# Expert weights fetched as pairs: one 2 MB transfer with 16 KB per partition in place of two of 1 MB

## The chip, the cores and the metric

The kernel runs on one core of one Trainium2 chip. The metric is the device time of one execution in microseconds (us). Before the change it is 2197.31 us, the median of three runs (2195.88, 2197.31 and 2199.11 us). For this kernel a difference of less than about 0.2% (4.4 us) can't be told from none.

## What is computed

The reference is a stack of transformer blocks over 256 tokens of width 1024, in float32. The first block has two layers. Each layer runs a hybrid mixer (latent attention, retention and a causal block attention) and then a feed-forward part: layer 0 a dense SwiGLU of inner width 2816, layer 1 a mixture of eight SwiGLU experts of inner width 3584. The second block follows with a feed-forward, a gated mixer with dilated attention, a cross attention to 256 memory rows and another feed-forward. The part that the change touches is this one:

```python
def moe_swiglu(x, w_router, w_gate, w_up, w_down):
    logits = (xt @ w_router).astype(jnp.float32)
    top_v, top_i = lax.top_k(logits, TOP_K)          # TOP_K = 2 of 8 experts
    top_w = jax.nn.softmax(top_v, axis=-1)
    ...
    for e in range(N_EXPERTS):
        y = y + gates[:, e:e + 1] * swiglu(xt, w_gate[e], w_up[e], w_down[e])
```

All eight experts' weights are read: 8 x 3 x 1024 x 3584 floats, 352 MB.

## The kernel before

All weights are laid out on the host as one stream of 504 chunks. A full chunk is a tile of 128 partitions x 2048 float32 (`CW`), 8 KB per partition and 1 MB in all. Chunks 72 to 407 (`AT["f1"]` is 72, `3 * U_MOE` is 336) are the experts': each expert has 14 units of 256 inner columns, and a unit takes three chunks, two that hold gate and up columns and one that holds down rows.

A chunk goes through four engines, in this order:

- SyncE (`load`, lines 345 to 349) brings chunk n into slot n % 6 of `raw` (`RAW` = 6 slots). It first waits until VectorE is done with chunk n - 6 (`lo_done`). The transfer's arrival adds 16 to the semaphore `landed` of that slot. In a feed-forward stage SyncE runs a loop whose body issues six transfers.
- ScalarE (`hi`, lines 1121 to 1125) waits for `landed` and for TensorE to be done with chunk n - 3 (`used`), and writes the rounded copy into slot n % 3 of `whi`.
- VectorE (`lo`, lines 1492 to 1496) subtracts that from the raw chunk into `wlo`, the remainder, and adds one to `lo_done`, which frees the raw slot.
- TensorE multiplies in three passes (`mm3`, lines 483 to 486): high by high, high times remainder and remainder times high. In the experts' stage a chunk is four 128 x 512 blocks, so twelve matmuls.

Within a unit (`unit` inside each engine's `experts`) TensorE runs `gate_up` on two chunks, `down` of the unit before on the third, and `turn`, two transposes (line 657) of the unit's activated product. ScalarE's order is: `hi` of two chunks, the SiLU (line 1227) once `gate_up` is done, `hi` of a third chunk, the copy of the transposed product (line 1233). VectorE's order is: `lo` of two chunks, the product (line 1647), `lo` of the third, the remainder of the transposed product (line 1653). All of these orders are fixed in the program, so what stands behind a waiting `hi` on ScalarE, or behind a waiting `lo` on VectorE, waits too. ScalarE and VectorE run two chunks ahead of the chunk that TensorE is at (`LEAD` = 2).

GpSimd brings the gathered token rows of each next expert in (`xs`, 512 KB) and stores the outputs of each one before (512 KB), on its own queue.

Of the kernel before, what the change touches and what calls it, by code (L numbers as in the profile page):

```python
# [24 lines left out]
P = 128  # L25
# [4 lines left out]
CW = 2048  # L30
RAW = 6
# [5 lines left out]
LB = 3 * UNROLL  # L37
# [18 lines left out]
U_MOE = NE * U_E  # L56
# [68 lines left out]
AT, WIDTH = {}, []  # L125
# [64 lines left out]
    raise KeyError((stage, kind))  # L190


class Chunk:


    def __init__(self, base, it=0):
        self.raw = base % RAW
        self.split = base % SPLIT
        self.width = WIDTH[base]
        self.base = base  # L200
        self.n = base + LB * it
        self.landed = 16 * (base // RAW + 1) + (16 * (LB // RAW)) * it


def in_chunk(l, c):

    return AT[f"in{l}"] + c if c < 4 else AT[f"inb{l}"] + c - 4
# [14 lines left out]
def program(nc, stream, x_in, mem_in, pos_in, consts, route_in, cols_in, rows_in, ws_in, blank_in, out):  # L222
    with ExitStack() as ctx:
        def sb(name, shape, dt=F32):
            return ctx.enter_context(nc.sbuf_tensor(name, shape, dt))
# [3 lines left out]
        def sem(name):  # L229
            if name not in sems:  # L230
                sems[name] = ctx.enter_context(nc.semaphore(name))
            return sems[name]
# [24 lines left out]
        raw = sb("raw", [P, RAW, CW])  # L257
# [53 lines left out]
        a = 2 * T * D  # L311
# [21 lines left out]
        landed = [sem(f"landed{n}") for n in range(RAW)]  # L333
        hi_done = sem("hi_done")
        lo_done = sem("lo_done")
# [8 lines left out]
        @block.sync  # L344
        def _(sp):
            def load(c):
                if not (isinstance(c.n, int) and c.n < RAW):
                    sp.wait_ge(lo_done, c.n - RAW + 1)
                sp.dma_start(raw[:, c.raw, 0:c.width], stream[c.n, :, 0:c.width]).then_inc(landed[c.raw], 16)

            for t in range(T):
                sp.wait_ge(sem(f"x_in{t}"), 16)
            n = 0
            while n < NCHUNK:
                if any(n == AT[f] for f in ("f0", "f1", "f2", "f3")):
                    name = next(f for f in ("f0", "f1", "f2", "f3") if n == AT[f])
                    loops = 3 * (U_MOE if name == "f1" else U_FF) // LB
                    with sp.Fori(0, loops) as it:
                        for j in range(LB):
                            load(Chunk(n + j, it))  # L360
                    n += loops * LB
                else:
                    load(Chunk(n))
                    n += 1
# [746 lines left out]
        def _(act):  # L1111
# [7 lines left out]
                act.wait_ge(sem("act_chain"), chained[0])  # L1119

            def hi(c):
                act.wait_ge(landed[c.raw], c.landed)
                if not (isinstance(c.n, int) and c.n < SPLIT):
                    act.wait_ge(used, c.n - SPLIT + 1)
                act.activation(whi[:, c.split, 0:c.width], raw[:, c.raw, 0:c.width], ACT.Copy).then_inc(hi_done, 1)  # L1125

            def advance(upto):

                while cursor[0] <= min(upto, NCHUNK - 1):
                    hi(Chunk(cursor[0]))  # L1130
                    cursor[0] += 1
# [45 lines left out]
            def ffn(name, units, scaled=None):  # L1177
                first_chunk = AT[name]

                def unit(u, base, it, chunks):  # L1180

                    n = base + LEAD
                    for j in range(chunks - 1):
                        if n + j < NCHUNK:
                            hi(Chunk(n + j, it))
                    act.wait_ge(used, base + LB * it + 2)
                    for t in range(T):
                        act.activation(sg[:, t, :], ps[t][:, 0:FU], ACT.Silu,  # L1188
                                       scale=rstd[:, t:t + 1] if scaled else 1.0).then_inc(unit_sem(name, "sg"), 1)
                    if n + chunks - 1 < NCHUNK:  # L1190
                        hi(Chunk(n + chunks - 1, it))
                    act.wait_ge(*at(name, "ut", u + 1))
                    act.activation(hth[:, 0:2, :], ps[2][:, :].rearrange("p (k s) -> p k s", k=2), ACT.Copy).then_inc(  # L1193
                        unit_sem(name, "hh"), 1)
# [186 lines left out]
            for l in range(DEPTH):  # L1381
# [12 lines left out]
                else:  # L1394
                    act.wait_ge(sem("rt_flag"), 1)
                    overfull = act.value_load(flag[0:1, 0:1], min_val=0, max_val=1)
                    n = cursor[0]
# [41 lines left out]
            for t in range(T):  # L1439
                m = act.activation(prob[:, t, :], r[:, t, 512:D], ACT.Square, accum_out=ss[:, 2 + t:3 + t])  # L1440
# [24 lines left out]
            for i in range(X_H):  # L1465
# [3 lines left out]
                for t in range(T):  # L1469
                    m = act.activation(prob[:, i % 2, t * S:(t + 1) * S], ps[2 + i % 2][:, t * S:(t + 1) * S], ACT.Exp,  # L1470
                                       bias=nmax[:, i, t:t + 1], scale=X_D ** -0.5, accum_out=rsum[:, i, t:t + 1])
# [727 lines left out]
def lay_out_stream(a):  # L2199

    big = np.zeros((NCHUNK, P, CW), np.float32)

    def project(name, w):
        n = AT[name]
        for c in range(0, w.shape[1], 512):
            part = w[:, c:c + 512]
            wide = part.shape[1]
            v = part.reshape(KD, P, wide).transpose(1, 0, 2)
            if wide == 512:
                big[n] = v[:, 0:4].reshape(P, CW)  # L2210
                big[n + 1] = v[:, 4:8].reshape(P, CW)
                n += 2
            else:
                big[n, :, 0:KD * wide] = v.reshape(P, KD * wide)
                n += 1

    def ffn(name, gate, up, down):

        units = gate.shape[0] * gate.shape[2] // FU
        per = units // gate.shape[0]  # L2220
        first_chunk = AT[name]
        for u in range(units):
            e, c = u // per, (u % per) * FU
            gu = np.concatenate([gate[e, :, c:c + FU].reshape(KD, P, FU), up[e, :, c:c + FU].reshape(KD, P, FU)], axis=2)
            v = gu.transpose(1, 0, 2)
            first = first_chunk + max(3 * u - 1, 0)
            big[first] = v[:, 0:4].reshape(P, CW)
            big[first + 1] = v[:, 4:8].reshape(P, CW)
            last = first_chunk + (3 * u + 4 if u < units - 1 else 3 * u + 2)
            big[last] = down[e, c:c + FU].reshape(2, P, D).transpose(1, 0, 2).reshape(P, CW)  # L2230

    first = np.cumsum([0, 256, 128, 32] + [320] * 7)
    parts = dict(zip(("ret q", "ret k", "ret v", "gate", "moba q", "moba k", "moba v"), first[3:]))

    def head_columns(part, n):
        return np.arange(parts[part] + HD * n, parts[part] + HD * (n + 1))

    order = [np.arange(C_PAIR)]
    for pair in PAIRS:
        order += [head_columns(f"{kind} {part}", n) for part in "qkv" for kind, n in pair]  # L2240
    order = np.concatenate(order + [head_columns("gate", n) for n in range(RET_H)])
    for l in range(DEPTH):
        w = a["w_in"][l][:, order]
        c = 0
        for g, wide in enumerate(IN_WIDTHS):
            v = w[:, c:c + wide].reshape(KD, P, wide).transpose(1, 0, 2)
            c += wide
            for j in range(2):
                big[in_chunk(l, 2 * g + j), :, 0:4 * wide] = v[:, 4 * j:4 * j + 4].reshape(P, 4 * wide)
        big[AT[f"uq{l}"], :, 0:1152] = a["w_uq"][l].reshape(2, P, 576).transpose(1, 0, 2).reshape(P, 1152)  # L2250
        big[AT[f"ukv{l}"], :, 0:768] = a["w_ukv"][l]
        v = a["w_o"][l].reshape(KD, P, D).transpose(1, 0, 2)
        n = AT[f"o{l}"]
        for part in range(2):
            big[n + part, :, 0:1536] = v[:, 0:3, 512 * part:512 * part + 512].reshape(P, 1536)
        big[n + 2] = v[:, 3:5].reshape(P, CW)
        big[n + 3] = v[:, 5:7].reshape(P, CW)
        big[n + 4, :, 0:1024] = v[:, 7]
    ffn("f0", a["ffn_w_gate"], a["ffn_w_up"], a["ffn_w_down"])
    big[AT["router"], :, 0:KD * NE] = a["router"][0].reshape(KD, P, NE).transpose(1, 0, 2).reshape(P, KD * NE)  # L2260
    ffn("f1", a["exp_w_gate"][0], a["exp_w_up"][0], a["exp_w_down"][0])
    ffn("f2", a["ffn1_w_gate_2"], a["ffn1_w_up_2"], a["ffn1_w_down_2"])
    project("in2", a["w_in_2"][0])
    project("out2", a["w_out_2"][0])
    project("wk", a["cross_wk_2"][0])
    project("wv", a["cross_wv_2"][0])
    project("wq", a["cross_wq_2"][0])
    project("xo", a["cross_wo_2"][0])
    ffn("f3", a["ffn2_w_gate_2"], a["ffn2_w_up_2"], a["ffn2_w_down_2"])
    return big  # L2270
# [35 lines left out]
```

## Time and profile before

| | us |
|---|---|
| median of three runs | 2197.31 |
| the profiled execution's own time | 2198.82 |
| its span, first to last instruction | 2197.0 |
| TensorE matmul busy | 2051.8 (93% of the span) |
| VectorE busy | 1516.8 (69%) |
| ScalarE busy | 1246.8 (57%) |
| weights' DMA queue (q1), share of 16 engines' span | 63.0% |

The times above come from one profiled execution. The page of the profile also has the span in 40 equal slices of 55 us. The experts' stage fills slices 10 to 27, about 540 to 1490 us from the start, and there the slices of the DMA engines read 9 tenths nearly throughout. Matmuls overlap in the records (each is listed as some 0.39 us long while the next one starts 0.23 us after it), so TensorE's busy time says whether it stands still and not how fast it could be.

### The profile page before, as it was taken

Reading aid. Unit: us, or ns where it says so; the run is one execution under the profiler, and the core shown is the slowest. Engines: PE = TensorE matmul, PEld = TensorE weight load, DVE = VectorE, ACT = ScalarE, POOL = GpSimd, SP = SyncE. Lnnn points to the kernel's source line nnn. Section 1 sums busy time; section 2 is a strip of 40 time slices with the busy share of each in tenths; the row PEclk is TensorE's granted clock in tenths of the full one; section 3 lists DMA queues with packets and bytes.
Section 4 is the critical chain, followed back from the end, with each engine's and each line's share of the span. In section 5 each row is a group of like instructions: output and inputs, shape, how many; then the busy total and the mean of one; then the engine's idle time right before and its main releaser. Section 6 shows DMA issues by size and latency. Waiting matters only on the chain.

```text
span 2197.0 us, 26792 instructions
## 1 busy us (share of the span) xinstructions
PE 2051.8 (93%) x9606; PEld 1700.9 (77%) x9606; DVE 1516.8 (69%) x1528; ACT 1246.8 (57%) x1302; POOL 67.8 (3%) x84
## 2 busy tenths in 40 slices
PE   6979998986999999899989999998999988989997
PEld 6858886876888888788878888876888766877886
DVE  5664455656889899799979899996555554545543
ACT  5544434544777777677767777765444543434443
POOL 1010000001000000000000000220000000000000
PEclk9989999996999999999999999998999977999999
DMA  7336554334999999899989999996555421434550
GB/s 306 125 129 245 188 174 141 116 116 164 374 370 388 375 381 380 331 371 383 374 336 378 380 375 364 406 362 224 195 190 191 163 106 69 161 106 153 191 191 19
DMA packets 78375, 548.77 MB, mean 250 GB/s; under 512 B 8960, under 2 KB 8960, under 8 KB 15840
## 3 DMA queue, kind: packets, MB, share of 16 engines
q1 hardware_dynamic: 72576, 519.77, 63.0%
q0 software_dynamic: 5712, 27.77, 3.4%
q8 instruction: 64, 1.05, 0.2%
q14 instruction: 23, 0.19, 0.0%
HBM read 540.68 MB, written 10.49 MB: 251 GB/s over the span
## 4 chain that ended last, share of the span: by engine, by line
PE 89%; DVE 6%; ACT 3%; issue 1%; DMA 1%; POOL 0%; DVEq 0%; ACTq 0%; SPq 0%; POOLq 0%
PE ps L484 27%; PE ps L486 27%; PE ps L485 27%; DVE wlo L1495 1%; PE ps L657 1%; ACT whi L1125 1%; PE ps L592 1%; PE ps L500 1%; DVE resid L1542 0%; PE ps L853 0%; DMA raw<-in_stream 0%; PE ps L874 0%; DVE r L1551 0%; DVE xtl L1509 0%; PE ps L742 0%
## 5 line engine op out<-in xcount | busy, mean ns | idle before, releaser
L1495 DVE TENSOR_TENSOR wlo<-raw,whi 128x2048 fp32r<-128x2048 f32 (+3 forms) x504 | 1142.6, 2271 | 370.0 <-ACT whi L1125 364.5
L1125 ACT ACTIVATE whi<-raw 128x2048 fp32r<-128x2048 f32 (+3 forms) x504 | 950.1, 1887 | 261.2 <-PE ps L486 256.8
L484 PE MATMUL ps<-whi,xth 128*128 128x512 f32 (+2 forms) x1872 | 748.9, 400 | 28.6 <-DVE wlo L1495 9.9
L486 PE MATMUL ps<-whi,xtl 128*128 128x512 f32 (+2 forms) x1872 | 729.5, 390 | 0.0
L485 PE MATMUL ps<-wlo,xth 128*128 128x512 f32 (+2 forms) x1872 | 728.4, 389 | 0.0
L484 PEld LDWEIGHTS ps<-whi,xth 128*128 128x128 f32 x1872 | 357.3, 191 | 101.8 <-issue 21.9
L486 PEld LDWEIGHTS ps<-whi,xtl 128*128 128x128 f32 x1872 | 356.6, 191 | 72.3
L485 PEld LDWEIGHTS ps<-wlo,xth 128*128 128x128 f32 x1872 | 357.9, 191 | 65.3
L484 PE MATMUL ps<-whi,hth 128*128 128x512 f32 (+2 forms) x736 | 287.4, 390 | 6.7 <-DVE htl L1607 4.5
L486 PE MATMUL ps<-whi,htl 128*128 128x512 f32 (+2 forms) x736 | 286.2, 389 | 0.0
L485 PE MATMUL ps<-wlo,hth 128*128 128x512 f32 (+2 forms) x736 | 285.1, 387 | 0.0
L484 PEld LDWEIGHTS ps<-whi,hth 128*128 128x128 f32 x736 | 138.6, 188 | 36.3 <-issue 5.6
L486 PEld LDWEIGHTS ps<-whi,htl 128*128 128x128 f32 x736 | 138.4, 188 | 28.2
L485 PEld LDWEIGHTS ps<-wlo,hth 128*128 128x128 f32 x736 | 138.7, 188 | 27.3
L1227 ACT ACTIVATE prob<-ps 128x256 f32<-128x256 f32 x112 | 43.1, 385 | 92.2 <-PE ps L486 92.2
L1233 ACT ACTIVATE hth<-ps 128x256 fp32r<-128x256 f32 x112 | 43.1, 384 | 85.8 <-PE ps L657 85.8
L1193 ACT ACTIVATE hth<-ps 128x512 fp32r<-128x512 f32 x33 | 19.7, 598 | 101.0 <-PE ps L592 101.0
L500 PE MATMUL ps<-cst,resid 128*128 128x128 f32 x112 | 24.0, 384 | 53.6 <-DVE resid L1542 51.5
L500 PEld LDWEIGHTS ps<-cst,resid 128*128 128x128 f32 x112 | 19.2, 199 | 58.7 <-DVE resid L1542 42.3
L1188 ACT ACTIVATE prob<-ps,rstd 128x256 f32<-128x256 f32 x44 | 18.4, 470 | 79.0 <-PE ps L486 79.0
L1607 DVE TENSOR_TENSOR htl<-ps,hth 128x512 fp32r<-128x512 f32 x33 | 22.8, 691 | 52.4 <-ACT hth L1193 52.4
L1647 DVE TENSOR_TENSOR probt<-prob,ps 128x256 f32<-128x256 f32 x112 | 46.5, 415 | 2.8 <-ACT prob L1227 2.8
(318 smaller groups left out, 1295.2 us busy)
## 6 DMA issues: line engine op xcount, KB each, us to landing
raw<-in_stream SPq DMA_DIRECT2D x481, 1024.0 KB, 6.6
raw<-in_stream SPq DMA_DIRECT2D x8, 768.0 KB, 4.4
bc<-in_rows POOLq DMA_DIRECT2D x5, 1024.0 KB, 5.1
slot_rows<-in_blank POOLq DMA_DIRECT2D x7, 512.0 KB, 9.5
kc<-slot_rows POOLq DMA_DIRECT2D x7, 512.0 KB, 8.6
sum_rows<-r POOLq DMA_DIRECT2D x7, 512.0 KB, 8.1
raw<-in_stream SPq DMA_DIRECT2D x4, 832.0 KB, 5.4
raw<-in_stream SPq DMA_DIRECT2D x4, 640.0 KB, 3.9
```

Source lines behind the costliest of these rows:

```text
L484: pe.matmul(o, ah, bh, start=start, stop=False, skip_group_check=True)
L485: pe.matmul(o, ah, bl, start=False, stop=False, skip_group_check=True)
L486: return pe.matmul(o, al, bh, start=False, stop=stop, skip_group_check=True)
L500: m = pe.transpose(ps[banks[k // 2]][:, (k % 2) * S + t * P:(k % 2) * S + (t + 1) * P], src[:, t, k * P:(k + 1) * P], ident)
L592: m = pe.transpose(ps[2][:, k * S + t * P:k * S + (t + 1) * P], hs[:, t, k * P:(k + 1) * P], ident)
L657: m = pe.transpose(ps[1][:, k * P:(k + 1) * P], hs[:, 0, k * P:(k + 1) * P], ident)
L1125: act.activation(whi[:, c.split, 0:c.width], raw[:, c.raw, 0:c.width], ACT.Copy).then_inc(hi_done, 1)
L1227: act.activation(sg[:, 0, :], ps[0][:, 0:FU], ACT.Silu).then_inc(sem("e_sg"), 1)
L1233: act.activation(hth[:, 0:2, 0:P], ps[1][:, 0:2 * P].rearrange("p (k s) -> p k s", k=2), ACT.Copy).then_inc(sem("e_hh"), 1)
L1495: dve.tensor_tensor(wlo[:, c.split, 0:c.width], raw[:, c.raw, 0:c.width], f32(whi[:, c.split, 0:c.width]), ALU.subtract).then_inc(lo_done, 1)
L1607: dve.tensor_tensor(htl[:, 0:2, :], ps[2][:, :].rearrange("p (k s) -> p k s", k=2), f32(hth[:, 0:2, :]), ALU.subtract).then_inc(unit_sem(n ...
L1647: dve.tensor_tensor(hs[:, 0, :], sg[:, 0, :], ps[0][:, FU:2 * FU], ALU.mult).then_inc(sem("e_h"), 1)
```

## The change

In the experts' stage SyncE issues one transfer for two neighbouring chunks (even n, odd n + 1), into two neighbouring slots of `raw`. On the host the chunks of the stage are rearranged in pairs, so that the 16 KB of one partition lie together in memory and the pair is one contiguous 2 MB. The loop of SyncE has three transfers in its body and no longer six. A pair has to wait for both of its slots, so it waits for chunk (n + 1) - 6 to be done, where chunk n alone waited for n - 6. Its arrival is counted on the even slot's semaphore alone, and `hi` of both chunks waits for that. Behind the stage the odd slots' semaphores are 56 arrivals lower, and `Chunk` counts that off. The number of slots, the orders on ScalarE, VectorE and TensorE, and all other stages stay.

```diff
@@ class Chunk
-        self.landed = 16 * (base // RAW + 1) + (16 * (LB // RAW)) * it
+        self.paired = PAIRED <= base < PAIRED + 3 * U_MOE
+        self.by = self.raw - self.raw % 2 if self.paired else self.raw
+        alone = self.raw % 2 == 1 and base >= PAIRED + 3 * U_MOE
+        self.landed = 16 * (base // RAW + 1 - alone * (3 * U_MOE // RAW)) + (16 * (LB // RAW)) * it
@@ SyncE
+            pairs = stream[PAIRED:PAIRED + 3 * U_MOE].rearrange("(m a) p c -> m (a p c)", a=2).rearrange(
+                "m (p n) -> m p n", p=P)
+
+            def load_pair(c, m):
+                sp.wait_ge(lo_done, c.n + 1 - RAW + 1)
+                sp.dma_start(raw[:, c.raw:c.raw + 2, :].rearrange("p a n -> p (a n)"), pairs[m]).then_inc(landed[c.raw], 16)
...
                         for j in range(LB):
-                            load(Chunk(n + j, it))
+                            if name != "f1":
+                                load(Chunk(n + j, it))
+                            elif j % 2 == 0:
+                                load_pair(Chunk(n + j, it), it * (LB // 2) + j // 2)
@@ ScalarE
-                act.wait_ge(landed[c.raw], c.landed)
+                act.wait_ge(landed[c.by], c.landed)
@@ host
+    pairs = big[PAIRED:PAIRED + 3 * U_MOE]
+    pairs[:] = pairs.reshape(-1, 2, P, CW).transpose(0, 2, 1, 3).reshape(pairs.shape)
```

`PAIRED` is `AT["f1"]`, 72.

## Rows read from the trace of the kernel before

**Rows 1.** Busy time by stretch of the experts' stage; "x" is the number of instructions.

```profile
core 0: us, PE busy (x) PEld busy (x) DVE busy (x) ACT busy (x) POOL busy (x), PEclk, DMA share, GB/s
600.00:700.00 100.00, 100.00 (x453) 82.22 (x452) 90.34 (x61) 76.16 (x62) 1.11 (x2) 1.00 0.99 379
...
800.00:900.00 100.00, 94.16 (x420) 77.08 (x420) 84.14 (x57) 69.46 (x57) 0.53 (x1) 0.97 0.96 370
```

**Rows 2.** Who waited for whom, 600 to 1450 us: total, times, longest.

```profile
DVE wlo L1495 <- ACT whi L1125: 93.3, 255, 7.8
...
ACT whi L1125 <- PE ps L486: 65.4, 92, 8.2
...
PE ps L484 <- issue: 6.1, 1, 6.1
PE ps L484 <- DVE wlo L1495: 5.8, 1, 5.8
```

**Rows 3.** The same view for the queue of SyncE.

```profile
SPq L349 <- DVE wlo L1495: 667.2, 293, 9.5
```

**Rows 4.** Line 349 (weights' transfers), issue to landing, 536 to 575 us, 13 transfers.

```profile
DMA to landing us min/median/max: 4.7/4.8/5.8
```

**Rows 5.** The same line, 600 to 1450 us, 293 transfers.

```profile
DMA to landing us min/median/max: 4.7/7.1/11.1
```

**Rows 6.** Busy time in two more stretches; columns as in rows 1.

```profile
900.00:905.00 5.00, 5.00 (x26) 4.09 (x24) 3.08 (x3) 3.71 (x3) 0.00 (x0) 1.00 0.07 18
...
1408.00:1430.00 22.00, 21.90 (x98) 17.59 (x97) 20.23 (x13) 16.41 (x14) 10.90 (x5) 1.00 1.02 422
```

**Rows 7.** DMA issues, 600 to 1450 us: count, KB each, median us to landing.

```profile
sum_rows<-r POOLq DMA_DIRECT2D x7, 512.0 KB, 8.1
kc<-slot_rows POOLq DMA_DIRECT2D x6, 512.0 KB, 8.6
```

**Rows 8.** VectorE in order of time: start, duration, instruction, idle before and releaser.

```profile
738.46 2.29 DVE L1495 TENSOR_TENSOR wlo<-raw,whi 128x2048 fp32r<-128x2048 f32 x1 [0.15 <-ACT whi L1125]
740.96 2.29 DVE L1495 TENSOR_TENSOR wlo<-raw,whi 128x2048 fp32r<-128x2048 f32 x1 [0.21 <-ACT whi L1125]
743.17 0.41 DVE L1647 TENSOR_TENSOR probt<-prob,ps 128x256 f32<-128x256 f32 x1
743.95 2.29 DVE L1495 TENSOR_TENSOR wlo<-raw,whi 128x2048 fp32r<-128x2048 f32 x1 [0.37 <-ACT whi L1125]
...
746.89 2.29 DVE L1495 TENSOR_TENSOR wlo<-raw,whi 128x2048 fp32r<-128x2048 f32 x1 [0.31 <-ACT whi L1125]
```

**Rows 9.** SyncE's queue in order of time, the one issue of that stretch.

```profile
740.93 0.33 SPq L349 DMA_DIRECT2D raw<-in_stream  x1
```

**Rows 10.** ScalarE in order of time, the chunks of rows 8 and the next.

```profile
736.52 1.91 ACT L1125 ACTIVATE whi<-raw 128x2048 fp32r<-128x2048 f32 x1
739.01 1.92 ACT L1125 ACTIVATE whi<-raw 128x2048 fp32r<-128x2048 f32 x1 [0.58 <-PE ps L486]
...
750.42 1.91 ACT L1125 ACTIVATE whi<-raw 128x2048 fp32r<-128x2048 f32 x1
```

**Rows 11.** TensorE in order of time: transposes, and first matmuls of chunks.

```profile
735.82 0.38 PE L657 MATMUL ps<-cst,probt 128*128 128x128 f32 x2
...
744.26 0.38 PE L657 MATMUL ps<-cst,probt 128*128 128x128 f32 x2
744.39 0.48 PE L484 MATMUL ps<-whi,xth 128*128 128x512 f32 x1
...
747.22 0.39 PE L484 MATMUL ps<-whi,xth 128*128 128x512 f32 x1
...
749.94 0.39 PE L484 MATMUL ps<-whi,hth 128*128 128x512 f32 x1
```

More of the change, by code:

```diff
@@ L190, in before @@
     raise KeyError((stage, kind))
+PAIRED = AT["f1"]
+assert PAIRED % RAW == 0 and 3 * U_MOE % RAW == 0
 class Chunk:
```

## The prediction

> **What bounds the kernel now.** I read the slices of the page first, then the stretches of the experts' stage, then the waits, and last the order in time of one piece of the stage. In the stretches the reader is to see that TensorE never stands still: 100.00 of 100 us busy between 600 and 700 us, while VectorE has 90 and ScalarE 76, and the DMA engines are busy 0.99 at 379 GB/s [rows 1]. So two resources are near their end at once, and the question is which one gives way. The waits answer it. Over 850 us TensorE has only two that matter, of 6.1 and 5.8 us, both near a return of the loop over expert pairs, and in the 5 us behind the first the DMA engines are busy 0.07 [rows 6], since all slots are full; no wait of ScalarE for a transfer is in the list at all, it waits for TensorE (65.4 us) [rows 2]. SyncE, on the other hand, waits for VectorE before each of its 293 transfers, 667.2 us in all [rows 3]: transfers start when a slot comes free and not a moment sooner. The stage is TensorE's, and the transfers are hidden as long as each lands before ScalarE wants it.
>
> **How much room the transfers have.** One piece of the stage shows it. Number the chunks by their `hi`: the one that starts at 736.52 is a; then a+1 at 739.01, and a+5 at 750.42 [rows 10]. `lo` of a runs from 738.46 to 740.75, and SyncE issues the transfer of a+6 at 740.93, 0.18 us later [rows 8, 9]. This a is odd, a+5 and a+6 are the two halves of a future pair, and the pair would be issued where a+6 is issued now, at 740.93. Chunk a+5 is wanted by its `hi` at 750.42. So a pair has 750.42 - 740.93 = 9.5 us to land, where a chunk alone had one slot's time more, about 2.8 us: a unit of three chunks lasts 744.26 - 735.82 = 8.44 us [rows 11], 2.81 us a chunk, which gives 12.3 us.
>
> If the `hi` is late, TensorE isn't late at once. I read its reserve as the time from the end of a `lo` to TensorE's first matmul on that chunk: `lo` ends 743.25, 746.24 and 749.18 [rows 8], first matmuls at 744.39, 747.22 and 749.94 [rows 11], so 1.14, 0.98 and 0.76 us for the three kinds of chunk. Behind the `hi` there are also the SiLU on ScalarE and the product on VectorE, which end at 743.58 for transposes at 744.26: 0.68 us, and this counts where the late chunk is the last before the SiLU. Added to 9.5, TensorE stands still only when a pair takes over 10.2 to 10.6 us from issue to landing. There is a second limit, the round trip of the slots. Three pairs are under way in six slots, so issue, landing, two `hi`/`lo` and the next issue must fit into 3 x 2 x 2.81 = 16.9 us. Without the landing that is 0.18 + 1.91 + 0.04 + 2 x 2.29 = 6.7 us, and 7.1 with a product (0.41) between; 9.8 to 10.2 us remain for a landing that is always that long. I take 10.2 as the point from which time is lost.
>
> **How long a pair takes to land.** No row has a 2 MB transfer. A 1 MB transfer into quiet engines takes 4.8 us [rows 4]; in the long run of the stage 7.1 us [rows 5], which is 7.1 / 2.81 = 2.5 transfers in flight and a queue of 2.3 us in front of each. The second megabyte takes at least 1.049 MB / 422 GB/s = 2.5 us, from the highest rate that the stage shows [rows 6], and at most the pace, 2.8 us. So below it is 4.8 + 2.5 = 7.3 us, above it 7.1 + 2.8 = 9.9 us. I take 9.3: nearer the upper end, because the queue in front of the transfers holds over nearly all of the 293, and lower than it by 0.6, because a pair is issued 5.6 us after the last one, when most of that one has been moved.
>
> 9.3 is under 10.2, so the ordinary pair costs nothing. What is late next are the pairs beside other traffic. GpSimd moves 7 + 6 transfers of 512 KB in the stretch [rows 7], each 0.524 / 422 = 1.2 us of all engines' time. A pair behind one lands at 10.5, 0.3 us past the point: 13 x 0.3 = 4 us, if each meets a pair at its worst. The longest landing now is 11.1, 4.0 over the median [rows 5]; a few such pairs would cost 3 us each, and after each the queue is shorter. I take 4 us for both kinds together.
>
> **The other parts.** SyncE issues 168 transfers fewer, 0.33 us each [rows 9], 55 us of a queue that waits for 667 us: nothing, since its waits hide it. The copy, the subtraction and the matmuls are the same in number and shape: nothing. The half of a pair that lands first is not available earlier than the other; that is in the 9.3 us already. The added wait stands at the head of ScalarE's queue; behind it are the SiLU and the second `hi`, whose reserves are counted above. Into the stage: the pairs are loaded during routing, when ScalarE's and VectorE's work on chunks is sparse, and landings of 4.8 us [rows 4] show quiet engines there; with 7.3 us a pair is still within 9.5. Out of the stage single transfers start as before, by the same waits. Nothing is given back either: TensorE's two standstills (6.1 and 5.8 us, and the lower clock beside one, 0.97 over its 100 us [rows 1]) are where the slots fill up behind them [rows 6].
>
> At one place a rule of the Trainium skill stands against the reading. Its page DMA: Bandwidth & Descriptors (section Specifications) gives about 358 GB/s as the limit of one core's share of the memory; if it bound here, a megabyte would take 2.93 us and the stage would already run at the memory's pace. The trace disagrees: 379 GB/s over 100 us and 422 over 22 us.
>
> The sum: +4 us on the profiled execution's 2198.8 (span 2197.0), or 2202.8. That execution is 1.5 us over the median of 2197.3, so in terms of the median it is 2201.3; I predict 2201.
>
> **The rivals.**
>
> (B) Slower: the landing of the pairs becomes the pace. Place: ScalarE's `hi` of the even chunk, waiting for `landed`. It decides from a landing of 10.2 us. For it speaks that the upper end (9.9) is 0.3 us from there, and that the DMA engines are 0.99 busy, so that any time in which they run dry between two pairs is hard to win back. Against it, that 422 GB/s have been seen where the pace needs 1.049 / 2.81 = 373. Price: 0.15 us over the point on average makes 168 x 0.15 = 25 us, so 2222; 0.05 gives 8 us, 0.3 gives 50.
>
> (C) Slower by more: runs of 16 KB are moved at a lower rate than runs of 8 KB. No row bears on it. The pace needs 373 GB/s, so a rate of 360 would make a pair 2.097 / 360 = 5.83 us against 5.62, 168 x 0.21 = 35 us: 2232, and more for less.
>
> (D) Faster: the two standstills of TensorE get shorter because fewer pieces of weights are queued in front of what it waits for there. They are 11.9 us together; half of it gone is 6 us: 2191. Against it speaks that nothing in the rows says that this waits for the DMA engines.
>
> (E) Faster by much: the fixed part of each transfer is saved. 4.8 us for one alone less 2.5 at full rate is 2.3 us, and 168 x 2.3 = 386 us would give 1811. Transfers overlap by 2.5 and TensorE waits for none, so I give it 1 in 100. The rule is on the same page of the Trainium skill (section Anatomy of one DMA: about 2.0 us fixed per transfer, plus the bytes at 436 GB/s); the 4.8 us agree with it to 0.4 us, and the waits show that the fixed part lies under other work.
>
> That the change doesn't do what it says, the runs being cut back into 8 KB pieces, leaves the later issue of the first half and so the forecast.
>
> **How the numbers follow.** The forecast (A, nothing lost in the ordinary pair, 0 to 4 us in the others) has 0.49. B has 0.34, C 0.09, D 0.07, E 0.01. What can be told from no change here is about 0.2%, 4.4 us. A lies almost wholly within that, I leave 0.03 of it above; B and C lie above, save for 0.02 of B; D lies below, save for 0.01, and so does E. So faster 0.07, same 0.49, slower 0.44. A's own range is 2196 to 2203. For 8 in 10 it reaches through B to 2232, and down to 2193; left out are C's larger values, B's top, and D and E.
>
> **What would show it.** If I am right, the profile of the changed kernel has 168 issues of 2048 KB with a median landing of 8.5 to 9.9 us, TensorE busy 100 in the stretches without the loop's return, and few or no waits of ScalarE for a transfer over the 0.7 us that are in reserve. A median landing near 7.3 would show the step on the queue wrong, without an effect on the time. B shows as waits of `hi` for the transfer at most even chunks and short waits of TensorE for VectorE all through the stage; C as that with a DMA rate under 373 GB/s and a share near 1; D as a shorter wait at the loop's two returns. I am wrong if landings over 10.2 us are more than one in ten.

## The result

The changed kernel takes 2207.58 us, the median of seven runs (2202.32 to 2209.74), against 2197.12 us for seven runs of the kernel before (2195.88 to 2199.11). The ratio is 1.0043, with a 95% interval of 1.0031 to 1.0055: slower by 9.4 us, between 7 and 12 (the two medians are 10.5 us apart). The time forecast was 2201 us and the range 2193 to 2232.

The table puts the profiled executions side by side. The last row is the experts' stage alone, from the end of VectorE's `lo` of chunk 75 to that of chunk 407, read from the two traces.

| us | before | changed |
|---|---|---|
| own time | 2198.82 | 2209.74 |
| span | 2197.0 | 2208.0 |
| TensorE busy | 2051.8 | 2056.6 |
| experts' stage | 959.4 | 969.8 |

So 10.4 of the 11.0 us by which the spans differ lie in the stage. The stretches of the changed kernel, in the columns of [rows 1, 6]:

```profile
600.00:700.00 100.00, 98.50 (x446) 80.36 (x445) 88.13 (x60) 74.54 (x60) 1.11 (x2) 1.00 0.97 374
800.00:900.00 100.00, 93.59 (x424) 76.14 (x423) 87.06 (x60) 72.42 (x58) 0.53 (x1) 0.98 0.97 368
900.00:905.00 5.00, 5.00 (x17) 4.01 (x18) 0.00 (x0) 0.76 (x1) 0.00 (x0) 0.72 1.01 396
```

Between 600 and 700 us TensorE now stands still for 1.5 us, where it didn't at all before, and the DMA engines have gone from 0.99 at 379 GB/s to 0.97 at 374. Between 800 and 900 us they went the other way, from 0.96 to 0.97; from 600 to 1390 us they are at 0.97 and 371 GB/s before and 0.96 and 368 GB/s now. (The third row is not at the same point of the work as its counterpart.)

The waits of the changed kernel, 600 to 1450 us, answering to [rows 2, 3]:

```profile
ACT whi L1142 <- DMA raw<-in_stream: 47.4, 46, 2.9
ACT whi L1142 <- PE ps L503: 45.2, 58, 8.7
...
PE ps L501 <- DVE wlo L1512: 12.2, 3, 5.8
...
PE ps L674 <- DVE probt L1664: 6.3, 8, 1.5
```

```profile
SPq L363 <- DVE wlo L1512: 745.5, 145, 13.1
```

(Lines have moved by 17: L1142 is the `hi` of L1125, L503 is L486, L674 the transposes of L657, L1664 the product of L1647.) The first row is new. ScalarE waits for a transfer 46 times in 145 pairs, 47.4 us together, and its waits for TensorE have shrunk from 65.4 to 45.2 us. TensorE feels a part of these 47 us. Its two standstills at the loop's returns (11.6 us together) are there as before; what is new stands in the last row above, the eight transposes that wait for the product on VectorE. (The kernel before has two such waits, of 1.7 us each, in the last expert; the changed kernel has them too, behind 1450 us.) Over the whole stage the standstills that TensorE's rows show rose from 15.5 to 22.2 us. Not all of the 10.4 us show as standstills: a unit grows by some 0.15 us more than the wait that is listed in it (by 1.68 for the wait of 1.50 below), which fits the 0.16 us by which matmuls overlap in the records, and what is left beyond that isn't broken down here.

The landings, first of the pairs in the first 40 us of the stage, then from 600 to 1450 us, answering to [rows 4, 5]:

```profile
DMA to landing us min/median/max: 7.7/9.3/9.9
```

```profile
DMA to landing us min/median/max: 7.6/9.7/12.2
```

And the page's list of issues, answering in part to [rows 7]:

```profile
raw<-in_stream SPq DMA_DIRECT2D x168, 2048.0 KB, 9.6
...
kc<-slot_rows POOLq DMA_DIRECT2D x7, 512.0 KB, 10.8
sum_rows<-r POOLq DMA_DIRECT2D x7, 512.0 KB, 11.2
```

One late pair, in order of time, ScalarE and then VectorE and TensorE of the changed kernel:

```profile
668.93 1.91 ACT L1142 ACTIVATE whi<-raw 128x2048 fp32r<-128x2048 f32 x1
673.72 1.92 ACT L1142 ACTIVATE whi<-raw 128x2048 fp32r<-128x2048 f32 x1 [2.88 <-DMA raw<-in_stream]
675.54 0.36 ACT L1244 ACTIVATE prob<-ps 128x256 f32<-128x256 f32 x1
```

```profile
675.67 2.29 DVE L1512 TENSOR_TENSOR wlo<-raw,whi 128x2048 fp32r<-128x2048 f32 x1 [2.15 <-ACT whi L1142]
677.88 0.41 DVE L1664 TENSOR_TENSOR probt<-prob,ps 128x256 f32<-128x256 f32 x1
```

```profile
678.35 0.44 PE L674 MATMUL ps<-cst,probt 128*128 128x128 f32 x2 [1.50 <-DVE probt L1664]
```

`hi` stands 2.88 us for the transfer. The SiLU behind it starts when `hi` ends and no longer when TensorE is done; the product is behind `lo` in the same way; and the transposes come 1.50 us late. A wait of 2.88 us on ScalarE cost TensorE 1.50. At 794 us it is 2.01 and 0.67, at 1290 us 2.16 and 0.82: about 1.35 us less each time.

### The profile page after: what moved, and what is told of

The parts are those of the page before. It is cut to its first block, busy times and chain, and to the rows that moved or that the text cites. A ratio compares the mean times of both kernels' runs of the same rounds, so it can differ in the third digit from the quotient of the medians.

```text
span 2208.0 us, 26188 instructions
## 1 busy us (share of the span) xinstructions
PE 2056.6 (93%) x9606; PEld 1700.9 (77%) x9606; DVE 1512.2 (68%) x1528; ACT 1248.1 (57%) x1302; POOL 69.1 (3%) x84
## 4 chain that ended last, share of the span: by engine, by line
PE 80%; DVE 8%; DMA 6%; ACT 4%; issue 2%; DVEq 0%; POOL 0%; ACTq 0%; SPq 0%; POOLq 0%
PE ps L501 24%; PE ps L503 24%; PE ps L502 24%; DMA raw<-in_stream 5%; DVE wlo L1512 3%; ACT whi L1142 2%; PE ps L674 1%; PE ps L609 1%; PE ps L517 1%; DVE resid L1559 1%; PE ps L870 0%; PE ps L891 0%; DVE r L1568 0%; DVE xtl L1526 0%; PE ps L759 0%
## 5 line engine op out<-in xcount | busy, mean ns | idle before, releaser
L1142 ACT ACTIVATE whi<-raw 128x2048 fp32r<-128x2048 f32 (+3 forms) x504 | 949.9, 1887 | 288.9 <-PE ps L503 237.4
L503 PE MATMUL ps<-whi,xtl 128*128 128x512 f32 (+2 forms) x1872 | 729.8, 390 | 0.0
L503 PEld LDWEIGHTS ps<-whi,xtl 128*128 128x128 f32 x1872 | 357.1, 191 | 72.6
L503 PE MATMUL ps<-whi,htl 128*128 128x512 f32 (+2 forms) x736 | 286.0, 389 | 0.0
L503 PEld LDWEIGHTS ps<-whi,htl 128*128 128x128 f32 x736 | 138.5, 188 | 28.3
L674 PE MATMUL ps<-cst,probt 128*128 128x128 f32 x224 | 43.4, 275 | 10.7 <-DVE probt L1664 10.7
```

The source lines that it names most:

```text
L503: return pe.matmul(o, al, bh, start=False, stop=stop, skip_group_check=True)
L674: m = pe.transpose(ps[1][:, k * P:(k + 1) * P], hs[:, 0, k * P:(k + 1) * P], ident)
```

## The experiments

All but the first row, the result above, were timed in five rounds beside the kernel before; a ratio is to the kernel before on the same chip. "Stage" is the time between the ends of the `lo` of chunks 75 and 407 in the profiled execution, less the 959.4 us of before. It is free of what varies outside the stage, but it is one execution, and that isn't always a typical one: the profiled execution of the changed kernel is 2.2 us above the median of its runs, that of e3 2.3 us below, that of e9 2.5 below, and that of e12b 10.1 below. Times are therefore judged by the ratios, and the traces are read for where and how.

| run | issue | per pair | `hi` waits for | ratio, 95% | stage |
|---|---|---|---|---|---|
| changed | late | 1 x 2 MB, 16 KB runs | both | 1.0043, 1.0031 to 1.0055 | +10.4 |
| e11_after_again | late | the same | both | 1.0051, 1.0037 to 1.0066 | +9.2 |
| e1_late_apart | late | 2 x 1 MB | its own | 1.0008, 0.9999 to 1.0017 | +0.2 |
| e2_early_joined | early | 2 x 1 MB | both | 1.0011, 1.0002 to 1.0020 | +0.3 |
| e3_late_joined | late | 2 x 1 MB | both | 1.0022, 1.0013 to 1.0031 | +3.0 |
| e4_one_transfer_8kb | late | 1 x 2 MB, 8 KB runs | both | 1.0039, 1.0026 to 1.0052 | +11.5 |
| e5_after_trimmed | late | as changed | both | 1.0046, 1.0033 to 1.0059 | +7.8 |
| e6_before_trimmed | early | as before | its own | 1.0001, 0.9992 to 1.0010 | -1.6 |
| e7_stores_in_four | late | as changed | both | 1.0061, 1.0048 to 1.0074 | +7.6 |
| e8_five_slots | 1 slot late | as before | its own | 1.0005, 0.9996 to 1.0014 | +1.1 |
| e9_four_slots | 2 slots late | as before | its own | 1.0082, 1.0065 to 1.0098 | +10.4 |
| e10_halves_of_partitions | late | 2 x 1 MB, 64 partitions | both | 1.2987, 1.2958 to 1.3016 | +631.4 |
| e12b_four_of_512kb | late | 4 x 512 KB, 4 KB runs | both | 1.0159, 1.0145 to 1.0173 | +24.8 |

**Taking the change apart: e1, e2, e3 and e4.** The change does three things: it issues the even chunk later, it makes the even chunk wait for the odd one's bytes, and it merges two transfers.

```diff
 # e1_late_apart, on the kernel before (SyncE, experts' stage)
+            def load_late(c, d):
+                sp.wait_ge(lo_done, d.n - RAW + 1)
+                for half in (c, d):
+                    sp.dma_start(raw[:, half.raw, :], stream[half.n, :, :]).then_inc(landed[half.raw], 16)
 # e2_early_joined, on the kernel before (ScalarE); e3_late_joined has both
                 act.wait_ge(landed[c.raw], c.landed)
+                if c.paired and c.raw % 2 == 0:
+                    act.wait_ge(landed[c.raw + 1], c.landed)
 # e4_one_transfer_8kb, on the changed kernel (and the host's rearrangement out)
-            pairs = stream[PAIRED:PAIRED + 3 * U_MOE].rearrange("(m a) p c -> m (a p c)", a=2).rearrange("m (p n) -> m p n", p=P)
+            pairs = stream[PAIRED:PAIRED + 3 * U_MOE].rearrange("(m a) p c -> m p a c", a=2)
```

> Two transfers of 1 MB per pair, both issued where the changed kernel issues its one of 2 MB, each counted and awaited by itself. Theory J (the even chunk is held back by the odd one's bytes: a pair takes 9.7 us to land where its first half is wanted after 9.5): the first half lands after some 7 us and is in time, the second after some 9.7 where it is wanted after 12.3, so the time of before, 2197 within 3 us, and no more waits of ScalarE for a transfer than a handful. Rival L (the later issue alone costs it, because the DMA engines run dry between two pairs and never win the time back): 2204 to 2210, as the changed kernel. Rival K (the long run of 16 KB or the size of the transfer costs it): 2197, as theory J; run e4_one_transfer_8kb tells K from J.

> The transfers of before, of 1 MB and issued as early as before, but ScalarE takes up the even chunk only when the odd one has landed too. Theory J: the odd chunk is issued 2.8 us after the even one and lands 7.1 us after that, 9.9 us of the 12.3 that the even chunk has; 2.4 us are left over, more than most of GpSimd's transfers add, so 2197 to 2200. If waiting for both halves were enough by itself, without the later issue, it would be 2204 to 2210. Rival L: 2197, since nothing is issued later.

> Two transfers of 1 MB per pair, issued together as in e1_late_apart, and ScalarE waits for both as in e2_early_joined: all of the change but the one long transfer. Theory J: as the changed kernel, 2204 to 2210, with landings of the second half near 9.7 us and some 50 waits of ScalarE for a transfer. Rival L: the same time as e1_late_apart. Rival K (size or run length): 2197.

> One transfer of 2 MB per pair at the changed kernel's time, from the layout of before, so in runs of 8 KB and not of 16 KB. Theory J and rival L: as the changed kernel, 2204 to 2210, median landing 9.7 us. Rival K, if it is the run length: 2197 to 2200, landings near 9.3 us or less.

The later issue alone costs nothing clear (1.0008), which ends rival L. Waiting for both halves alone costs about as little (1.0011, with an interval that begins just above one). The two together cost 1.0022, and merging them into one transfer brings 1.0039 in runs of 8 KB and 1.0043 and 1.0051 in runs of 16 KB. So theory J holds for e1 and e2 and for about half of the size; for e3 it missed, with 2201.5 us for 2204 to 2210, last bytes at 8.3 us for 9.7, and 6 waits for some 50. Whether the late issue and the joint wait need each other isn't shown either: 1.0022 is hardly more than the sum of what each costs alone. The run length is not what costs: e4 and the changed kernel lie in each other's intervals. That one 2 MB transfer is worse than two of 1 MB issued together is rival K by size; it is right for that part and wrong for e3, which it had at 2197. The intervals of e3 and of both runs of the changed kernel do not overlap, or only touch at 1.0031; e3's and e4's do overlap.

The landings agree. From the issue of a pair to its last byte, chunks 120 to 385, worked out from issues and landings of each trace, 133 pairs:

| run | median | 95 of 100 are below | over 10.2 us |
|---|---|---|---|
| e1_late_apart | 8.5 | 10.3 | 7 |
| e3_late_joined | 8.3 | 10.1 | 6 |
| e4_one_transfer_8kb | 9.0 | 11.3 | 24 |
| changed | 9.7 | 10.9 | 27 |
| e11_after_again | 9.3 | 10.9 | 20 |
| e5_after_trimmed | 9.4 | 10.4 | 18 |
| e7_stores_in_four | 8.9 | 10.1 | 4 |
| e12b_four_of_512kb | 9.9 | 11.4 | 46 |

Not every late pair costs. What counts is which chunk of a unit the pair's even chunk is, the one whose `hi` waits. In the changed kernel, of the same 133 pairs:

| even chunk of the pair | pairs | over 10.2 us | TensorE stands still behind it |
|---|---|---|---|
| the last before the SiLU | 44 | 9 | 8 times, 6.4 us |
| one of the two others | 89 | 18 | once, 0.6 us |

For the first kind TensorE's wait is the landing less 10.0 to 10.15 us in six of the eight cases: 11.64 us gives 1.50, 10.91 gives 0.82, 10.77 gives 0.67. (One of the eight pairs was under 10.2, at 9.9 us.) Of the second kind 17 late pairs of 18 cost nothing. In the other runs the first kind has 8 late pairs (e11), 8 (e4), 7 (e5), 15 (e12b), 1 (e3) and none (e7). In e4 TensorE also stands still four times, 1.9 us in all, behind pairs of the second kind.

In e3 the waits of ScalarE for a transfer are under a quarter of the changed kernel's (600 to 1450 us):

```profile
PE ps L497 <- DVE wlo L1510: 12.9, 3, 5.8
ACT whi L1140 <- DMA raw<-in_stream: 10.9, 6, 3.6
PE ps L670 <- DVE probt L1662: 4.1, 3, 2.2
```

e1 has as many late last bytes as e3, and its stage grows by 0.2 us against 3.0: where the even chunk does not wait for them they do little harm. In e3's trace nearly all of the 3.0 us lie in one unit, near 1426 us, where GpSimd's gathers at the end of the stage are just over; its execution was one of the faster ones, so the trace doesn't show where the median one loses its 4.8 us.

**GpSimd's traffic: e5, e6 and e7.** In the changed kernel's trace, half of the stage's loss (5.1 us) lies in the third unit of experts 1 to 7, where GpSimd stores the outputs of the expert before (3.2 in the trace of e11, the same kernel again). I took that for the cause.

```diff
 # e5_after_trimmed on the changed kernel, e6_before_trimmed on the kernel before
-                    pool.dma_start(xs, slot_rows[e * P:(e + 1) * P, :])
+                    pool.dma_start(xs[:, 0:64], slot_rows[e * P:(e + 1) * P, 0:64])
-                    pool.dma_start(sum_rows[e * P:(e + 1) * P, :], r[:, e % 2, :])
+                    pool.dma_start(sum_rows[e * P:(e + 1) * P, 0:64], r[:, e % 2, 0:64])
 # e7_stores_in_four, on the changed kernel
+                    for i in range(4):
+                        cut = slice(256 * i, 256 * i + 256)
+                        pool.dma_start(sum_rows[e * P:(e + 1) * P, cut], r[:, e % 2, cut]).then_inc(sem("y_out"), 16)
+                        pool.wait_ge(sem("y_out"), 16 * (4 * e + i + 1))
```

> The changed kernel with GpSimd's traffic in the experts' stage cut to a sixteenth: of the gathered rows of each next expert and of each stored output only 64 of 1024 columns are moved (those numbers are left out of the result, and 7 blank stores of 512 KB are added in layer 0). Theory G (the stage loses where a pair meets GpSimd's stores and loads): the 5 us at the third unit of each expert go, and about 3 us stay at the gathers of the last expert; against e6_before_trimmed 1.001 to 1.003. Rival H (GpSimd's transfers are no matter; the pairs are late on their own): 1.004 against e6_before_trimmed, as the changed kernel against the one before.

> The kernel before with the same traffic left out. Both theories: as the kernel before, 2197 within 4 us; it has 2.4 us of room or more per chunk and loses nothing to these transfers. It is what e5_after_trimmed is held against.

> The changed kernel with each 512 KB store of an expert's outputs cut in four of 128 KB, each issued when the one before has landed. Theory G: each piece takes 0.3 us of the DMA engines and not 1.2 at once, so the 5 us at the third unit mostly go and 2202 to 2205 is left. Rival H: nothing, 2204 to 2210. If the loss is proportional to the bytes and not to how densely they come, nothing either.

Theory G falls. Without the traffic the third units lose 0.5 us and no longer 5.1, as it said, and yet the ratio is 1.0046 and e6's 1.0001: nothing came back. (What e5 leaves in place are the gathers at the end of the stage; in the last expert it is 2.6 us behind e6, of 9.4 in the stage.) The pairs are still late, only elsewhere (600 to 1450 us of e5):

```profile
DMA to landing us min/median/max: 7.5/9.4/11.1
```

```profile
ACT whi L1145 <- DMA raw<-in_stream: 32.3, 30, 1.8
...
PE ps L677 <- DVE probt L1667: 2.0, 7, 0.5
```

It has 30 waits for a transfer where the changed kernel's trace has 46, and a median of 9.4 for 9.7; but e11, the changed kernel again with all its traffic, has 27 waits and 9.3, so that is no effect of the traffic. The stores decided where lateness showed, and not how much there was. Cut in four, they move the loss out of the third units too (0.1 us left), and the kernel is no faster, 1.0061. Its landings are earlier (median 8.9), and no pair of the kind that costs is late between chunks 120 and 385. Its 7.6 us in the stage lie elsewhere: 2.3 us in the units with the loop's returns and 3.9 in the last expert. Why it loses there, and the rest of its time, stays open.

Run e6, the kernel before with the same traffic left out, shows what the traffic does to single transfers (600 to 1450 us):

```profile
DMA to landing us min/median/max: 4.6/4.9/10.5
```

Without GpSimd's 13 large transfers the median landing of 1 MB falls from 7.1 to 4.9 us, as into quiet engines, at the same pace of use. The queue in front of the transfers of before is what GpSimd's transfers leave behind. The pairs land in 9.4 us without that traffic and in 9.7 and 9.3 with it, so what makes them late is their own.

**The room between landing and need: e8 and e9.**

```diff
 # e8_five_slots: later = 1 in the experts' stage; e9_four_slots: later = 2
-                    sp.wait_ge(lo_done, c.n - RAW + 1)
+                    sp.wait_ge(lo_done, c.n - RAW + 1 + later)
```

> The kernel before with each transfer of 1 MB in the experts' stage issued one slot later. It has 9.5 us to its hi, 10.2 with TensorE's reserve, for landings with a median of 7.1: 3.1 us of room, where the changed kernel has 0.5 and e9_four_slots 0.3. Theory M (what costs is the room between landing and need): nothing, 2197 within 4 us. If every later issue cost its part (half of what e9_four_slots lost): 2201 to 2209.

> The kernel before with each transfer of 1 MB in the experts' stage issued two slots later, as if raw had four slots there. It has 12.3 - 2 x 2.8 = 6.7 us to the start of its hi, 7.4 with TensorE's reserve, for a landing that has a median of 7.1 when there is no hurry and 4.8 in quiet engines: about the margin of the changed kernel (10.2 against 9.7) and without a large transfer. Theory M (what costs is the margin, wherever it comes from): a loss of 5 to 25 us, 2202 to 2222. Rival K2 (what costs is the size of the transfer): 2197 to 2200.

Both times came out as theory M has them. With 1 MB transfers and nothing joined, one slot less costs nothing (1.0005), two cost 1.0082. The landings of e9, 600 to 1450 us, and ScalarE's and TensorE's waits:

```profile
DMA to landing us min/median/max: 4.7/5.5/10.6
```

```profile
ACT whi L1125 <- DMA raw<-in_stream: 29.5, 34, 2.3
...
PE ps L484 <- DVE wlo L1495: 9.2, 7, 5.8
```

One thing in the expectation was wrong: the landing isn't 7.1 us there but 5.5, 1.9 us inside the 7.4. So by its median e9 has more room than the changed kernel, and it loses more (17 us by the medians of the runs, for 10.5): the margin of the median doesn't tell the loss. The tail tells that there is one. Over its limit of 7.4 us lie 23 of 266 landings of e9 (9 of 100); over 10.2 us lie 5 of 266 in e8, and 27 of 133 in the changed kernel. It doesn't tell how much: the share is smaller in e9 and the loss larger.

**Why one transfer is later than two: e10, e12b and e11.**

```diff
 # e10_halves_of_partitions, on the changed kernel (hi waits for both counts)
+                for i in range(2):
+                    half = slice(64 * i, 64 * i + 64)
+                    sp.dma_start(raw[half, c.raw:c.raw + 2, :].rearrange("p a n -> p (a n)"), pairs[m][half]).then_inc(landed[c.raw + i], 16)
 # e12b_four_of_512kb, on e3_late_joined (hi waits for all four counts)
+                    for i, count in enumerate((landed, landed_second)):
+                        cut = slice(CW // 2 * i, CW // 2 * (i + 1))
+                        sp.dma_start(raw[:, half.raw, cut], stream[half.n, :, cut]).then_inc(count[half.raw], 16)
```

> The changed kernel with its transfer of 2 MB issued as two of 1 MB at once, one for partitions 0 to 63 and one for 64 to 127, both in runs of 16 KB; ScalarE waits for both. Theory N (a transfer of 2 MB lands later than two of 1 MB issued together, which is why e3_late_joined lost half as much): as e3_late_joined, ratio 1.001 to 1.003, and the second lands some 8.3 us after the first is issued. Rival R (it is the run of 16 KB and, in e4_one_transfer_8kb, something else of its access pattern): as the changed kernel, 1.004, landings near 9.7. Rival Q (e3_late_joined and the changed kernel don't differ): between them, no telling apart.

> The changed kernel once more, beside e10_halves_of_partitions on the same chip. All theories: ratio 1.003 to 1.0055, median landing of the pairs 9.3 to 9.9 us.

> As e3_late_joined (all of a pair issued at the changed kernel's time, ScalarE waits for all of it), but in four transfers of 512 KB, each half the columns of one chunk in runs of 4 KB. Theory N (the fewer and larger the transfers that carry the same 2 MB, the later its last byte): no later than e3_late_joined, 8.3 us or less to the last byte in the median, ratio 1.000 to 1.0025. Rival S (the two chunks as separate transfers are what matters, a finer cut is a cost again through four issues of 0.33 us): 1.003 or more. If it comes out like the changed kernel (1.004 to 1.005), what e3_late_joined gained is not a matter of the number of transfers.

e10 says nothing on its question, since something larger hides it, which is told below. e11 repeats the changed kernel. e12b refutes theory N: four transfers are not earlier than two but later (a median of 9.9 us to the last byte for 8.3), and the time is 1.0159. Its DMA engines are full (0.99 busy at 368 GB/s from 600 to 700 us), and it has 53 waits for transfers where the changed kernel has 40 (600 to 1390 us):

```profile
ACT whi L1151 <- DMA raw<-in_stream: 58.4, 53, 3.2
```

A piece of 4 KB takes the engine 176 ns on average in its trace, so 352 for 8 KB, against 333 in e3 with pieces of 8 KB; and the fourth issue comes 1.6 us after the first, the second in e3 0.5 us after it. So the best of the forms tried is two transfers of 1 MB. Why one of 2 MB lands 0.7 us later than these two (e4, with the same runs of 8 KB) is left open.

## Why the prediction came out as it did

It was right by its range, and its likeliest case was wrong: forecast A had the ordinary pair free of cost and 4 us in all, a time of 2196 to 2203, and gave 0.49 to no visible change. What came is 9.4 us, in rival B's direction and between A and B's 25. Two of its signs failed with it: TensorE isn't busy for 100 of 100 us away from the loop's returns (98.50), and ScalarE has 46 waits for a transfer and not a few.

- **What bounds the kernel.** Right. ScalarE never waited for a transfer before, and a later issue of a single chunk by a whole slot is free (e8).
- **The room of 9.5 us, and 10.2 to 10.6 with TensorE's reserve.** Right, and by the path that it named. At 673 us a `hi` held up by 2.88 us, through the SiLU and the product, makes the transposes 1.50 us late, behind a pair that took 11.64 us; the point from which time is lost is near 10.1 us, for 10.2. What the prediction didn't use is that this holds for one pair in three. For the others it had 10.5 to 10.6, and it took 10.2 for all; 18 of the others were later than 10.2, and only one of them made TensorE wait.
- **The landing of 9.3 us.** Close, 9.7 in the one profile and 9.3 in the other, and partly by luck, since two errors cancel. It was worked out from the queue of before, 2.3 us, as if the pace made it; it is GpSimd's doing (e6), and two transfers of 1 MB, with the same bytes at the same time, land at 8.3 (e3). Against that, one large transfer is later than its bytes are, by 0.7 (e4) to 1.4 us, and the prediction had no term for it. Merging is about half of the whole loss (1.0022 against 1.0043).
- **"I take 4 us for both kinds together".** This is the step that failed, the term of the sum that was mis-sized: 10.4 us in the stage. It made lateness the business of GpSimd's 13 transfers and of a few outliers, and called the ordinary pair free, because 9.3 is under 10.2. But the landings spread, from 7.6 to 12.2, and 20 and 15 of 100 were over 10.2 (27 and 20 of 133); eight of those 27 made TensorE wait, by 0.2 to 1.5 us each. With the spread of before in view (4.7 to 11.1 about a median of 7.1 [rows 5]) that could have been seen: the prediction set its own mark at one in ten, and it was passed. GpSimd's part, 4 us by the sum, is not what is lost: without those 13 transfers the loss is the same (e5).
- **Rival B.** Its mechanism is what happened, in a mild form: waits at 46 of 145 pairs, not at most of them, and TensorE's waits in some units, not in all. The 0.15 us a pair, for which it gave 2222, was too high; 10.4 / 168 is 0.06, near the 0.05 for which it gave 8 us.
- **Rival C**, runs of 16 KB: wrong, e4 has 8 KB and the same time. A piece of 16 KB takes 611 ns, one of 8 KB 309.
- **Rivals D and E:** the two standstills of TensorE are 11.6 us together in the changed kernel's trace and 13.3 in e11's, for 11.9 [rows 2], and nothing of a fixed part came back. The rule of the Trainium skill that is named at E (DMA: Bandwidth & Descriptors, section Anatomy of one DMA) is given there for transfers that GpSimd issues. SyncE's take 4.8 us for 1 MB [rows 4], where an estimate by that page gives 4.4.
- **SyncE's 168 issues less**, priced at nothing: its waits only grew, from 667 to 746 us. The stages before and behind: 10.4 of 11.0 us are in the stage, so they cost nothing either.

## What to carry to other kernels

Where transfers are hidden already, fewer and larger ones have nothing to save, and a pair that has to wait for two free slots and is usable only as a whole gives up room twice: one slot's time at its issue, and the second half's bytes at its end. Compare the room with the tail of the landings and not with their median; ten to twenty in a hundred over the limit went with a measurable loss here, though TensorE was spared about 1.35 us of each wait. Ask also which of the transfers is the one with the least reserve behind it: here one pair in three made nearly all of TensorE's waits. And a place where stalls gather in a trace is not yet their cause: remove it and see whether the time moves.

## What the runs showed of the hardware

**Half of the partitions, half of the rate.** e10 moves the same bytes in the same run length as the changed kernel, in two transfers at once that each go to 64 partitions. Its stretch from 1000 to 1100 us, and the landings of its transfers from 700 to 1700 us:

```profile
1000.00:1100.00 100.00, 72.49 (x267) 55.75 (x266) 51.82 (x37) 42.53 (x36) 0.53 (x1) 0.86 1.01 225
```

```profile
DMA to landing us min/median/max: 7.2/18.2/24.8
```

The DMA engines are busy 1.01 of the time and move 225 GB/s, where the changed kernel moves 374 at 0.97. A piece of 16 KB takes 1191 ns in the median (700 to 1700 us) and not 611. The two transfers didn't add up to one of 128 partitions; the rate was held to about half, and they came one behind the other, the second landing 4.8 us after the first in the median. At 225 GB/s the 352 MB of the experts take 1566 us, and the stage took 1591, so the transfers are its pace. The Trainium skill (DMA: Bandwidth & Descriptors, section Rules for kernel authors) says not to split a transfer into partition halves since they serialize, and to use one of 128 partitions. The trace agrees, and shows what it costs here: 1.30 times the whole kernel's time.

**A landing is no constant of the transfer.** Median landings of 1 MB at nearly the same pace of use: 7.1 us with six slots, 7.1 with five, 5.5 with four, and 4.9 with six slots and without GpSimd's large transfers (e6). In the kernel before the median is 7.0 to 7.8 us in every 50 us from 610 to 1110, though GpSimd's transfers start 47 to 72 us apart: with DMA engines that are 0.99 busy, the queue isn't worked off between two of them.

**Six slots where five do.** e8 runs with the sixth slot's time unused and is not measurably slower (1.0005, 0.9996 to 1.0014); by that its 8 KB per partition could be had for something else in this stage, which no run tried.
